# First attention: the product with the values issued whole in every second round

## The reference

```python
def block_attention(q, k, v):
    ...
    def one_block(qb):                      # 128 queries
        s = jnp.einsum("bqkgd,bskd->bkgqs", qb, k).astype(jnp.float32)
        p = jax.nn.softmax(s, axis=-1).astype(v.dtype)
        return jnp.einsum("bkgqs,bskd->bqkgd", p, v)
```

## Time and profile before

| | |
|---|---|
| median of 3 runs | 3461.07 us (3458.13 to 3461.18) |
| profiled execution, first to last instruction | 3460.9 us |
| TensorE busy | 3361.4 us, 97% |
| VectorE busy | 2208.2 us, 64% |
| ScalarE busy | 1435.1 us, 41% |
| GpSimd busy | 1121.9 us, 32% |
| mean granted clock of TensorE | 0.990 |

### The profile page before, as it was taken

The page is one execution under the profiler, slowest core; times in us unless marked ns, Lnnn a source line. Parts: engine busy times, 40 slices in busy tenths (PEclk is TensorE's granted clock), DMA queues, the critical chain, the costliest instruction groups (busy, mean ns, idle before and its releaser), DMA issues.

```text
span 3460.9 us, 44771 instructions
## 1 busy us (share of the span) xinstructions
PE 3361.4 (97%) x16616; PEld 2710.6 (78%) x16616; DVE 2208.2 (64%) x2246; ACT 1435.1 (41%) x1901; POOL 1121.9 (32%) x644
## 2 busy tenths in 40 slices
PE   8899899999999999999999999999889999999998
PEld 6677777888888868888877777777668878888886
DVE  8896968777773474322277888888856574444434
ACT  5688835444441142333223443344453353333213
POOL 2000028888832212111111111111112276766222
PEclk9999999999999999999999999999999999999999
DMA  4210221222252112111111111111122212123322
GB/s 143 62 44 19 73 88 66 84 85 79 85 196 95 47 43 92 36 42 36 36 49 43 37 42 35 38 42 36 43 79 85 79 61 91 74 90 121 134 88 83
DMA packets 59167, 242.52 MB, mean 70 GB/s; under 512 B 6592, under 2 KB 6592, under 8 KB 53312
## 3 DMA queue, kind: packets, MB, share of 16 engines
q1 hardware_dynamic: 59072, 241.22, 19.7%
HBM read 194.53 MB, written 41.42 MB: 68 GB/s over the span
## 4 chain that ended last, share of the span: by engine, by line
PE 81%; DVE 12%; issue 3%; ACT 3%; DMA 0%; POOL 0%; DVEq 0%; POOLq 0%; ACTq 0%
PE ps L506 45%; PE ps L1457 24%; PE ps L2696 2%; PE ps L2708 2%; PE ps L2685 1%; PE ps L2846 1%; PE ps L2859 1%; DVE conv_acc L2310 1%; PE ps L529 1%; DVE t_wide L1094 1%; PE ps L2798 1%; PE ps L2853 1%; PE ps L2832 1%; DVE small L2350 1%; PE ps L2794 1%
## 5 line engine op out<-in xcount | busy, mean ns | idle before, releaser
L477 POOL TENSOR_TENSOR w_lo_part<-w_raw,w_hi_part 128x1024 fp32r<-128x1024 f32 x162 | 404.5, 2497 | 1739.0 <-ACT w_hi_part L460 1739.0
L506 PE MATMUL ps<-h_hi_part,w_hi_part 128*128 128x512 f32 x1904 | 625.4, 409 | 34.9 <-POOL w_lo_part L477 12.4
L506 PE MATMUL ps<-h_lo_part,w_hi_part 128*128 128x512 f32 x1904 | 596.5, 394 | 0.0
L506 PE MATMUL ps<-h_hi_part,w_lo_part 128*128 128x512 f32 x1904 | 594.9, 393 | 0.0
L460 ACT ACTIVATE w_hi_part<-w_raw 128x1024 fp32r<-128x1024 f32 x180 | 189.1, 1051 | 720.0 <-PE ps L506 632.4
L506 PEld LDWEIGHTS ps<-h_hi_part,w_hi_part 128*128 128x128 f32 x1904 | 348.1, 191 | 130.4 <-issue 37.2
L506 PEld LDWEIGHTS ps<-h_lo_part,w_hi_part 128*128 128x128 f32 x1904 | 361.7, 190 | 78.5 <-issue 0.3
L506 PEld LDWEIGHTS ps<-h_hi_part,w_lo_part 128*128 128x128 f32 x1904 | 361.4, 190 | 78.7
L2310 DVE SCALAR_TENSOR_TENSOR conv_acc<-u_pad,cols,conv_acc 128x1024 f32<-128x1024 f32 x232 | 307.4, 1325 | 19.4 <-DVE conv_acc L2310 2.8
L2149 DVE TENSOR_TENSOR residual<-residual,ps 128x1024 f32<-128x1024 f32 (+1 forms) x60 | 73.2, 1221 | 268.7 <-PE ps L506 262.2
L506 PE MATMUL ps<-u_hi,w_hi_part 128*128 128x512 f32 x736 | 232.0, 390 | 0.0
(11 more groups left out here) (446 smaller groups left out, 6583.1 us busy)
## 6 DMA issues: line engine op xcount, KB each, us to landing
w_raw<-in_w SPq DMA_DIRECT2D x226, 512.0 KB, 3.3
w_raw_odd<-in_w SPq DMA_DIRECT2D x46, 512.0 KB, 3.9
u_spill<-ffn_u SPq DMA_DIRECT2D x46, 512.0 KB, 3.0
u_wide<-u_spill SPq DMA_DIRECT2D x23, 1024.0 KB, 9.2
residual<-in_x SPq DMA_DIRECT2D x4, 1024.0 KB, 9.0
both_halves<-q_chan SPq DMA_DIRECT2D x16, 256.0 KB, 4.3
x_again<-in_x SPq DMA_DIRECT2D x8, 512.0 KB, 3.9
residual<-in_x SPq DMA_DIRECT2D x2, 2048.0 KB, 7.2
```

Of the source, the lines that this page charges most:

```text
L477: pool.tensor_tensor(WLO[:, slot], WRAW[:, slot], f32(WHI[:, slot]), ALU.subtract).then_inc(w_ready, 1)
L506: last = pe.matmul(PS[:, ps, b * HALF:(b + 1) * HALF], st[:, slot, k, :], at(mv, k, b), start=(k == 0 and n == 0), stop=(k == nk - 1 and n ...
```

## The change

Before, every round from 2 on issued half of a product with the values. Now even rounds issue none and odd rounds issue all eight steps of it. The product is that of the same q in both versions, and it ends in the same round. The number of instructions, their operands and the orders of the other engines stay as they are.

```diff
                 turn(g)
                 if g >= 62:
                     gate_pe(pe, 0, g - 62)
-                if g >= 2:
-                    pv(g // 2 - 1, range(4 * (g % 2), 4 * (g % 2) + 4))
+                if g >= 2 and g % 2:
+                    pv(g // 2 - 1, range(QT))
             gate_pe(pe, 0, 2)
             pv(31, range(QT))
             gate_pe(pe, 0, 3)
```

## The result

The changed kernel takes 3465.72 us (median of 21 runs, 3462.87 to 3467.15), the kernel before 3460.29 us (21 runs, 3456.14 to 3463.87). The ratio is 1.0014, with a 95% interval from 1.0008 to 1.0020: slower by 5.4 us between the medians, 0.16%, and by 0.14% as the ratio of the comparison gives it (from 0.08 to 0.20%, about 2.8 to 6.9 us). It is slower, clear of noise, and just inside the 0.2% that I set as the bound. I had forecast 5.4 more; that the tenth fits is luck.

A forecast was written before the change was run, and what follows sets the result against it. TensorE was taken to bound the kernel. 26 pairs at 0.22 us gave 5.7; with 0.9 - 1.1 - 0.15 that was +5.4 us, so 3466.5 us, range 3457 to 3472.

The forecast's parts named there:

- The loop over slot 0 and the loop over VectorE: Odd rounds: transposes wait for ScalarE's copy (3.16 us) and VectorE's scaling (3.13); new wait of 0.36 a pair.
- S: TensorE's scores part of a round, taken as 0.89 us.
- T: TensorE's eight transposes of a round, taken as 1.02 us.
- The price of the release: Waiting transposes start 1.14 us after ScalarE's copy began, or 0.81 after VectorE's scaling began.
- The saving of 0.15 by the whole product: Each pair of rounds: a whole product takes 1.90 us against 2.05 for two halves.
- The forecast by that rule, faster: Rival, TensorE in the attention: fewer mode changes save time and no wait comes, 5.1 us faster; chance 0.09.
- T gives way to S in 1.02: Changed order: scores follow the transposes after 1.02 us, as the product did; any difference is taken up by the wait.
- The start, +0.9: Up to round 6 VectorE is late; the whole product then ends 0.9 us later than the half, carried on.
- The turns of a head pair, -1.1: The product's wait of 0.36 us for the finished head pair's copy goes away, three times: -1.1.
- The end: Last rounds: no difference from scores to transposes of round 62, then one product whole instead of halved, -0.15 us.
- No loss to the pair of rounds 10 and 11: VectorE has two long operations there, so the pair is tight; nothing was allowed for it.
- The delay passes through: After the attention, TensorE's own progress releases weights and inputs, so the 5.4 us delay should reach the end.

The follow-up runs named there:

- e3: The changed kernel with ScalarE's copy in two halves and, in odd rounds 9 to 61, VectorE's scaling ahead of the next maximum: 3455.64 us, ratio 0.9986.
- e5: The kernel before, product in halves, with ScalarE's copy in two halves and VectorE's scaling ahead of the next maximum in odd rounds: 3458.45 us, ratio 0.9993.
- e4: The kernel before with its product split into one step in even rounds and seven in odd ones: 3462.80 us, ratio 1.0007.
- e7: The changed kernel with the product still in halves in rounds 2 to 7, whole from round 8: 3465.43 us, one run.

## Why the prediction was right, point by point

- *The loop over slot 0 and the loop over VectorE.* Forecast 3.16 and 3.13 from S; the weights of T came at 3.17. Relieving one left a pair of 6.06 (VectorE holds) and of 6.09 (the slot holds), as against 6.09 with both; the two loops are 0.02 to 0.03 apart, in the order that I gave. The trace names VectorE in 25 of 26 waits, although the slot is the later: at 0.03 us the name of the releaser was no guide here, and the distance from each release to T was.
- *The price of the release.* I took 1.14 from the copy to T from the start of T's weights; to its matmuls it is 1.17. T then gives way to the product after 0.99 or 1.00, not after 1.02. The two errors nearly cancel, and the product came at 4.20 instead of 4.18. That the pair is 6.09, the very value, is helped by this and by the 0.01 that I added.
- *The saving of 0.15 by the whole product.* Forecast from one product; in the chain of the changed kernel every product of 32 records takes 1.90. It stands alone in e3 (5.73) against e5 (5.87), 0.14. In e4, where the product is split unevenly and no part is saved, the parts still take 0.37 + 1.68 = 2.05. The Trainium skill (TensorEngine Tiling (Array Packing), Key Properties) states that a change of tiling mode drains TensorE. The traces agree with it, with about 0.15 us of a pair for one change fewer; no run shows the drain itself. The forecast by that rule, faster, was wrong for this edit and right once the wait was gone.
- *T gives way to S in 1.02.* Measured 161.86 to 162.88. It was hidden behind the wait, and counts only in e3.
- *The start, +0.9.* Measured +0.90, and taken back by e7. The steps fit as well: counted from T(2), T(5) stands at 8.88 (before 8.87), T(6) at 12.70 (12.00), T(7) at 15.00 (14.94) and T(8) at 18.78 (17.88).
- *The turns of a head pair, -1.1.* Before, the three pairs there take 6.22, 6.23 and 6.24 against 5.87; after, 6.10, 6.14 and 6.10. T(8) to T(60) grew by 4.61, which is 26 x 0.22 - 1.1.
- *The end.* T(60) to T(62) takes 5.38 in both, as forecast, though I gave no working for the 6.28 from S(62). T(62), forecast some 5.5 later, comes 5.5 later counted from T(2). Behind it I forecast -0.15, and measured is -0.31. I had counted only the shorter product. But a gate product now gives way to T(63) after 1.48 (308.18 to 309.66), where it gave way to the half product after 1.57 (303.26 to 304.83), and T(63) to the next gate product after 0.80 instead of 0.85.
- *No loss to the pair of rounds 10 and 11.* It took 6.09: right to allow nothing.
- *The delay passes through.* The medians differ by 5.4, the attention by 5.2. Shown within the error of the medians, about 2 us.

What had the least ground in the prediction was the sum itself: each term was good to some hundredths, but 26 pairs multiply it.

## What to carry to other kernels

When parts of a tightly packed engine's work are joined, look at what stood between two uses of the same buffer: the joined part was the cover of a copy, and the distance left (here 1.91 us of a needed 2.27) is the whole effect. A packed order has several loops of nearly the same length, so work out all of them before relieving one; here either relief alone gave nothing, and both turned a loss of 5.4 us into a gain (4.7 us by the medians, 2.7 in the trace of the attention). When two releases come this close, don't go by the name of the releaser: compare the distance from each release to the start with a wait where only one of them can hold. A saving that a wait hides (one change of mode fewer, 0.15 us) isn't lost, and here one step of eight between the two uses was enough to remove nearly all of the wait.

## What the runs showed that I had not expected

ScalarE's copy in two halves (0.60 and 0.59 long, 0.49 apart) costs little over the whole one (1.02 to 1.03 long): the second ends 1.08 after the first began. ScalarE's next instruction starts 0.95 to 0.98 after the first half in 34 of 47 rounds of the copy in halves (up to 1.09 in the others), against about 0.92 after a whole copy. So here a split copy releases half a PSUM slot 0.4 us earlier, mostly at 0.03 to 0.06 us of ScalarE's time.
